# Summing the squares of a norm on GpSimd instead of VectorE, in a TensorE-bound diffusion backbone

## The reference

```python
def rms_norm(x, g):
    xf = x.astype(jnp.float32)
    y = xf * lax.rsqrt(jnp.mean(xf * xf, axis=-1, keepdims=True) + NORM_EPS)
    return (y * g.astype(jnp.float32)).astype(x.dtype)

def ada_pre(h, g, shift, scale):
    return rms_norm(h, g) * (1.0 + scale) + shift

def swiglu(u, w_in, w_out):
    gate, val = jnp.split(u @ w_in, 2, axis=-1)
    return (jax.nn.silu(gate) * val) @ w_out

h_lat = h_lat + 0.5 * m_lat[2] * swiglu(ada_pre(h_lat, norm_g[l, 0], m_lat[0], m_lat[1]),
                                        ffn_w_in[l, 0], ffn_w_out[l, 0])
...
return rms_norm(h_lat, final_g)
```

## Time and profile before

| | |
|---|---|
| median of 3 runs | 2142.89 us |
| the profiled execution | 2142.82 us, of which the span from first to last instruction is 2141.1 us |
| granted TensorE clock, mean over the span | 0.982 of 2.4 GHz |
| busy: PE, DVE, ACT, POOL | 96%, 56%, 30%, 4% of the span |
| chain that ended last, by engine | PE 86%, DVE 7%, ACT 3%, DMA 2% |
| 49 adds of squares on DVE (L791) | 0.68 us for 128x512, 0.41 for 128x256 |
| 16 mask products on POOL | 13.4 us |
| DMA | 272.55 MB, mean 127 GB/s |

### The profile page before, as it was taken

How to read it: one execution, slowest core, us unless ns; L and a number is a source line. 1 busy time by engine, 2 the same in 40 slices (tenths; PEclk the granted TensorE clock), 3 DMA queues, 4 the chain that set the end, 5 groups by cost and what they waited for, 6 DMA issues and landing times.

```text
span 2141.1 us, 25318 instructions
## 1 busy us (share of the span) xinstructions
PE 2045.5 (96%) x9780; PEld 1609.6 (75%) x9780; DVE 1200.0 (56%) x1606; ACT 652.8 (30%) x669; POOL 83.9 (4%) x153
## 2 busy tenths in 40 slices
PE   6789999999998999999989999999999999799999
PEld 2358888786885676888868688888866667398998
DVE  2566767537556757676753776423373235765445
ACT  2342222224222214222212422222244344444333
POOL 0000000000000000000000000000000000100000
PEclk9899999999999999999999999999999998899999
DMA  6625555422221012555542165322311213034553
GB/s 214 258 66 190 196 196 187 147 98 79 93 84 59 1 63 87 196 196 196 177 157 98 59 206 186 118 98 98 127 70 64 74 60 128 20 119 149 185 177 118
DMA packets 47079, 272.55 MB, mean 127 GB/s; under 512 B 5229, under 2 KB 5869, under 8 KB 22893
## 3 DMA queue, kind: packets, MB, share of 16 engines
q1 hardware_dynamic: 27870, 195.21, 25.7%
q0 software_dynamic: 19152, 76.55, 10.8%
HBM read 270.69 MB, written 1.05 MB: 127 GB/s over the span
## 4 chain that ended last, share of the span: by engine, by line
PE 86%; DVE 7%; ACT 3%; DMA 2%; issue 1%; DVEq 0%; ACTq 0%; POOLq 0%
PE ps L1243 24%; PE ps L1244 24%; PE ps L1245 24%; PE ps L1520 3%; PE ps L1530 2%; PE ps L1236 2%; DMA ada_raw<-ada_stream_dram 1%; DVE tn L778 1%; PE ps L1592 1%; DVE act_lo L764 1%; PE ps L1439 1%; PE ps L1675 1%; DVE w_lo L701 1%; PE ps L1578 1%; ACT w_hi L374 1%
## 5 line engine op out<-in xcount | busy, mean ns | idle before, releaser
L1243 PE MATMUL ps<-act_hi,w_hi 128*128 128x512 f32 (+1 forms) x2728 | 990.4, 363 | 31.7 <-DVE act_lo L831 16.0
L1244 PE MATMUL ps<-act_lo,w_hi 128*128 128x512 f32 (+1 forms) x2728 | 982.8, 360 | 0.0
L1245 PE MATMUL ps<-act_hi,w_lo 128*128 128x512 f32 (+1 forms) x2728 | 982.4, 360 | 0.0
L701 DVE TENSOR_TENSOR w_lo<-w_raw,w_hi 128x2048 fp32r<-128x2048 f32 x172 | 394.0, 2291 | 516.7 <-ACT w_hi L374 516.7
L1243 PEld LDWEIGHTS ps<-act_hi,w_hi 128*128 128x128 f32 x2728 | 518.8, 190 | 127.3 <-DVE act_lo L764 13.8
L1245 PEld LDWEIGHTS ps<-act_hi,w_lo 128*128 128x128 f32 x2728 | 518.8, 190 | 77.1
L1244 PEld LDWEIGHTS ps<-act_lo,w_hi 128*128 128x128 f32 x2728 | 519.1, 190 | 75.7 <-issue 1.0
L374 ACT ACTIVATE w_hi<-w_raw 128x2048 fp32r<-128x2048 f32 x172 | 329.0, 1913 | 643.6 <-PE ps L1245 643.6
L723 DVE SCALAR_TENSOR_TENSOR ada_prod<-ada_w,cond_bc 128x1024 f32<-128x1024 f32 x120 | 146.3, 1219 | 11.4 <-DMA ada_w<-ada_rows_dram 11.4
L723 DVE SCALAR_TENSOR_TENSOR ada_w<-ada_w,cond_bc 128x1024 f32<-128x1024 f32 x120 | 146.3, 1219 | 0.0
L417 ACT ACTIVATE silu_g<-ps 128x1024 f32<-128x1024 f32 (+1 forms) x44 | 40.5, 920 | 307.3 <-PE ps L1245 307.3
(11 more groups left out here) (198 smaller groups left out, 1163.1 us busy)
## 6 DMA issues: line engine op xcount, KB each, us to landing
w_raw<-w_stream_dram SPq DMA_DIRECT2D x172, 1024.0 KB, 4.8
ada_w<-ada_rows_dram POOLq DMA_DIRECT2D x120, 512.0 KB, 3.8
ada_raw<-ada_stream_dram POOLq DMA_DIRECT2D x12, 1024.0 KB, 7.2
bd<-bd_dram SPq DMA_DIRECT2D x4, 768.0 KB, 6.2
edecay<-log_decay_dram SPq DMA_DIRECT2D x1, 2048.0 KB, 20.7
h<-tokens_dram SPq DMA_DIRECT2D x1, 2048.0 KB, 8.7
wg<-wg_dram SPq DMA_DIRECT2D x3, 512.0 KB, 4.8
w3aug<-w3aug_dram SPq DMA_DIRECT2D x1, 1040.0 KB
```

What stands on the lines that cost most here:

```text
L701: dve.tensor_tensor(w_lo[:, g % 2, :], w_raw[:, g % 2, :], w_hi[:, g % 2, :].bitcast(F32), ALU.subtract).then_inc(w_lo_done, 1)
L1243: pe.matmul(out, wh, xh, start=start, stop=False)
L1244: pe.matmul(out, wh, xl, start=False, stop=False)
L1245: return pe.matmul(out, wl, xh, start=False, stop=stop)
```

## The change

The 42 adds of norms 1 to 6 move from DVE's program to GpSimd's. The adds of norm 0 stay on DVE. GpSimd's loop over the row loads is cut in three, for tiles 2 to 49, 50 to 97 and 98 to 119, and the adds stand between the pieces: norms 1 and 2 behind the first, norm 3 behind the second, norm 4 behind the third, norms 5 and 6 behind the mask products. All semaphores keep their counts.

```diff
@@ block.gpsimd @@
-            with pool.Fori(1, ADA_TILES // 2) as q:
-                for s in range(2):
-                    pool.wait_ge(adaw_used, 4 * q - 2 + 2 * s)
-                    pool.dma_start(ada_w[:, s],
-                                   dram["ada_rows"][bass.ds(2 * q + s, 1)].rearrange("a p k -> (a p) k")
-                                   ).then_inc(adaw_loaded[s], 16)
-
+
+            def row_tiles(first, last):
+
+                with pool.Fori(0, (last - first) // 2) as i:
+                    for s in range(2):
+                        pool.wait_ge(adaw_used, 2 * first - 2 + 2 * s + 4 * i)
+                        pool.dma_start(ada_w[:, s],
+                                       dram["ada_rows"][bass.ds(first + s + 2 * i, 1)].rearrange("a p k -> (a p) k")
+                                       ).then_inc(adaw_loaded[s], 16)
+
+            def add_squares(n, cols):
+
+                for m in range(1, KT):
+                    pool.wait_ge(sq_ready, 8 * n + m + 1)
+                    if m > 1:
+                        pool.wait_ge(sq_added, 7 * n + m - 1)
+                    pool.tensor_tensor(sq_sum[:, cols], sq[:, 0, cols] if m == 1 else sq_sum[:, cols],
+                                       sq[:, m % 2, cols], ALU.add).then_inc(sq_added, 1)
+
+            row_tiles(2, 50)
+            add_squares(1, ALLC)
+            add_squares(2, ALLC)
+            row_tiles(50, 98)
+            add_squares(3, ALLC)
+            row_tiles(98, ADA_TILES)
+            add_squares(4, ALLC)
...
+            add_squares(5, LATC)
+            add_squares(6, LATC)
@@ block.vector, out_proj, rest @@
                         last.then_inc(h_ready, 1)
-                        if m >= 2:
-                            add_squares(o + 1, m - 1, cols)
-                    add_squares(o + 1, KT - 1, cols)
```

## The result

The changed kernel takes 2173.05 us, median of four runs (2166.89 to 2176.18), against 2142.16 for the kernel before (four runs). The ratio is 1.0138, 95% interval 1.0124 to 1.0153: slower by 31 us. That lies inside the forecast range of 2150 to 2176, near its upper end and 9 us above its centre, 2164. The profiled execution is the slowest of the four, 2176.18 us with a span of 2174.5.

What follows compares the result with a forecast made beforehand. TensorE, busy 96%, was taken as the bound, with fillers ending last in the six chains. Later column sums (16.2 us) plus lower clock (5.2) gave 21.4 on 2142.8, so 2164 us; range 2150 to 2176.

Steps and rivals of the forecast that it cites:

- Bound and slack: In the chain between sub-layers fillers end last; adds have about 0.1 us slack, limiting any gain; VectorE's free time brings nothing.
- The loads: GpSimd's row loads, tiles 2 to 119, in three loops instead of one: cost 0.
- An add of 128x512 on GpSimd: Each moved 512-column add takes 1.3 us, 1.38 with the hop; bounds 0.72 and 1.44.
- Taking turns: In chains 1 to 5 VectorE's weight split and GpSimd's adds hold each other off; one add takes about 3.3 us.
- The column sums: TensorE's column sums start later in the six chains: 3 x 3.4 + 3.2, +2.5, +0.3, sum 16.2 us.
- The clock: TensorE, idle before the column sums, drops its clock: 0 to 2.8 us a chain, 1.3 taken for four long norms, +5.2.
- No taking turns: Rival: the split delays only an add starting after it, or none; +6.5 us, no clock loss, 2149; chance 0.08.
- Updates of `h` caught too: Rival: VectorE's updates of h also take turns with GpSimd's adds, about 2.1 us per tile; about 2183; chance 0.07.
- GpSimd keeps up: Rival: adds within 1.04 us each, not held by the split, stay covered by fillers; 2143; chance 0.04.

## Why the prediction was right, point by point

**Bound and slack.** Right. The fillers covered the adds with 0.1 us to spare in the long norms. No gain came from VectorE's free time, and the time grew as soon as the adds were later than the fillers.

**The loads.** Priced at 0, and the loops alone measured 1.0004 with an interval across 1. In the changed kernel the load of tile 50, the first behind the adds, is issued 3.41 us after VectorE begins on tile 48, against 3.03 before; tile 98 is at 3.03 in both. VectorE still begins tile 50 at nearly the same distance, 10.23 us against 10.19, so the 0.4 us cost nothing.

**An add of 128x512 on GpSimd.** Forecast 1.3 us between bounds of 0.72 and 1.44, by the fixed part of VectorE's adds; measured 1.27 to 1.31 undisturbed. The hop between adds that depend on each other was put at 0.08 by the mask products and is 0.13 to 0.14. The Trainium skill's GPSIMD Engine Reference (3.1) gave an estimate of 1.33, which the trace bears out to 5%.

**Taking turns.** Right, with place and size: the split enters while add 5 runs, add 6 is 3.14 us long (forecast about 3.2, "one add of about 3.3"), the split is longer by 0.50 (2.78 for 2.28), most of the 0.63 us that add 5 still had to run when it began. Moving the split away makes both normal. In norm 5 one add of 2.60 us (forecast 2.7).

**The column sums.** Forecast +3.4, +3.2, +3.4, +3.4, +2.5, +0.3, sum 16.2; measured +3.5, +3.3, +3.6, +3.5, +2.7, +0.6, sum 17.2. The missing 1.0 us fits the hop, which was too short by 0.05 to 0.06 at each of the adds in a row, about 0.3 us a norm; adds of 1.27 to 1.31 instead of 1.3 took part of it back in the long ones.

**The clock: the term that was mis-sized.** The prediction took 1.3 us for each of four long norms, 5.2 in all, "the middle" between 0 and 2.8. Measured are 13.0 and 12.7 in two profiles. Three things were off. First, the clock did not miss a chain: it fell in norms 1 to 5, in both profiles. Second, the upper end was too low: at the low clock not only the fillers and `ones` but also the column sums take longer. In norm 3 that is 0.76 us (1.74 for 0.98), beside 2.12 for the fillers (4.40 for 2.28) and 0.45 for `ones`, and a whole fall costs 3.3 us instead of 2.8. Third, norm 5 with 2.4 us of idle time was left out and lost 1.65. With these sizes the sum is 16.2 + 13 = 29, and 2172. The range held because its upper end had been made from a full fall in five norms, not because 1.3 us was a good middle. The mechanism itself is shown: filling the idle time took away 12 us by the medians of one set, 2170.08 to 2158.15.

The middle also rested on a reading that is not right. The trace of the kernel before has not one idle stretch of TensorE of about this length, but four between 2.5 and 3.5 us. The other three, each with the granted clock of a window behind it:

```profile
646.97 1.94 PE L1508 MATMUL ps<-ident,scratch 128*128 128x128 f32 x8 [3.46 <-ACT zt L556]
647.00:650.00 3.00, 3.00 (x10) 0.50 0.76 303
...
660.62 1.07 PE L1508 MATMUL ps<-ident,scratch 128*128 128x128 f32 x8 [2.97 <-ACT zt L556]
660.62:664.00 3.38, 3.38 (x14) 1.00 0.00 0
...
1942.58 0.43 PE L1243 MATMUL ps<-act_hi,w_hi 128*128 128x256 f32 x1 [2.58 <-DVE w_lo L701]
1942.58:1945.00 2.42, 2.42 (x12) 0.54 0.56 125
```

With the 3.25 us of the earlier trace rows that is a low clock behind three of four, one of them behind 2.58 us. Read this way, a loss in most of the norms, the fifth included, was the better forecast.

**The rivals.** No taking turns: out, by the slow add and by its cure. Updates of `h` caught too: out, 480 ns against 477, and GpSimd's adds beside them take 1.28 to 1.31. The Trainium skill (SBUF — State Buffer, on the shared port pair) names only VectorE operations with two SBUF inputs or in a 2-port mode as rivals of GpSimd. The trace now agrees for an operation with one input in PSUM, 480 ns beside the adds. GpSimd keeps up: out; it would have needed 1.04 us an add.

What stays open is what sets off a fall of the clock when the idle time is short. With 1.62 us of it one program lost the clock behind norm 1 and kept it behind norm 3; with 1.72 us, norm 0 lost it in one profile of nine. Nor does a longer stretch always bring a fall: 2.97 us before 660.62 and, in the second profile of the changed kernel, 2.59 us before 1963.45 had none behind them.

## What to carry to other kernels

Before moving work to an idle engine, ask what ends last at that place: here it was filler work, so the relief was worth nothing and only the slower engine's lateness could show. Then look at what the relieved engine does next. It reached its next two-input operation earlier, exactly when GpSimd needed to read SBUF, and that one meeting cost as much as the whole difference in pace. And look at what runs behind a new wait of TensorE. Here waits of 2.7 to 3.5 us cost once for themselves and once more for what followed at the lower clock, and waits of 1.6 us did so only sometimes; filling them gave the second part back.

## What was not expected of the hardware

- The clock fell after an idle stretch of 1.6 us in norms 1 and 4 with the split moved, and after 1.72 us in norm 0 of the same profile. Before the prediction only a stretch of 3.25 us was weighed. In the changed kernel all ten idle stretches ahead of the column sums of norms 1 to 5 (two profiles, 2.66 to 3.49 us) had a fall behind them.
- At the low clock the column sums, eight matmul records of a single column, take 1.74 us instead of 0.98. At the full clock their eight weight loads alone take 0.97 us of the timeline's 1.05 in norm 1, so work that streams next to nothing is slowed as well.
- The start of the program, ahead of norm 0, differs between executions of the same program: 117.04 and 123.86 us. That is more than a small change of the kernel is worth (4 to 5 us for the fewer fillers), so a difference in the span has to be looked for at its place first.
